# A two-layer transformer kernel: the per-layer embedding product computed in the opening and kept in device memory, and x turned by products with a diagonal

## The reference

```python
cs = silu(c); mod = cs @ w_ada + b_ada              # shift1, scale1, ... of 1024 each
h = rms_norm(x, norm1_g) * (1 + scale1) + shift1     # rms_norm scales a row by 1/sqrt(mean(x*x)+eps)
proj = h @ w_in                                      # first layer: queries, keys, values, gates
...
x = x + mixed @ w_o                                  # second layer, "out2"
h2 = rms_norm(x, norm_mlp)
x = x + square(relu(h2 @ w_up)) @ w_down             # second layer, "mlp"
gate = sigmoid(rms_norm(x, norm_ple) @ w_ple_gate)
x = x + gate * (p_l @ w_ple)                         # p_l: 512 x 256, w_ple: 256 x 1024
```

## Time and profile before

| what | value |
|---|---|
| median of 3 runs | 2037.22 us (2035.78 to 2039.25) |
| the profiled execution | 2035.74 us |
| its span | 2033.9 us |
| PE busy | 1983.1 us, 97% |
| DVE, ACT, POOL busy | 1071.8, 805.8, 95.8 us |
| first of the 40 slices, PE busy | 6 tenths |
| the chain that ended last | PE 88%, DVE 6%, ACT 3%, DMA 1% |
| moved by DMA | 195.65 MB, 291 and 321 GB/s in slices 1 and 2, mean 96 |

### The profile page before, as it was taken

The page is one execution under the profiler, slowest core; times in us unless marked ns, Lnnn a source line. Parts: engine busy times, 40 slices in busy tenths (PEclk is TensorE's granted clock), DMA queues, the critical chain, the costliest instruction groups (busy, mean ns, idle before and its releaser), DMA issues.

```text
span 2033.9 us, 24084 instructions
## 1 busy us (share of the span) xinstructions
PE 1983.1 (97%) x9148; PEld 1599.4 (79%) x9148; DVE 1071.8 (53%) x1669; ACT 805.8 (40%) x1341; POOL 95.8 (5%) x116
## 2 busy tenths in 40 slices
PE   6999999999999999999999999999999999999998
PEld 4778777888888888877777777777778888888887
DVE  6686867456443544556363535666654453443355
ACT  4343556534221343333232323577742432322242
POOL 0140000011000000200000000000000100000010
PEclk9999999999999999999999999999999999999999
DMA  8842222123323332332322221212132233323221
GB/s 291 321 165 84 63 72 74 63 86 86 103 79 101 91 102 78 109 102 64 98 68 91 74 89 55 64 48 61 42 104 93 85 102 104 103 82 103 93 93 63
DMA packets 196487, 195.65 MB, mean 96 GB/s; under 512 B 8192, under 2 KB 170616, under 8 KB 194360
## 3 DMA queue, kind: packets, MB, share of 16 engines
q1 hardware_dynamic: 192928, 174.88, 27.9%
q0 software_dynamic: 3280, 19.67, 2.5%
q10 hardware_dynamic: 200, 0.06, 0.0%
HBM read 192.50 MB, written 2.10 MB: 96 GB/s over the span
## 4 chain that ended last, share of the span: by engine, by line
PE 88%; DVE 6%; ACT 3%; DMA 1%; issue 1%; SPq 0%; DVEq 0%; ACTq 0%
PE bank L735 45%; PE bank L700 4%; PE bank L1224 4%; PE bank L974 4%; PE bank L813 4%; PE bank L799 3%; PE bank L1477 3%; PE bank L1297 3%; PE bank L1029 2%; PE bank L1201 2%; PE bank L958 1%; PE bank L1212 1%; PE bank L924 1%; PE bank L1244 1%; PE bank L1164 1%
## 5 line engine op out<-in xcount | busy, mean ns | idle before, releaser
L1601 ACT ACTIVATE w_hi<-raw 128x2048 fp32r<-128x2048 f32 (+4 forms) x165 | 285.6, 1731 | 435.3 <-PE bank L735 300.6
L2357 DVE TENSOR_TENSOR w_lo<-raw,w_hi 128x2048 fp32r<-128x2048 f32 (+4 forms) x163 | 337.3, 2069 | 162.4 <-ACT w_hi L1601 160.6
L735 PE MATMUL bank<-h_hi,w_hi 128*128 128x512 f32 x864 | 338.5, 392 | 3.4 <-DVE w_lo L2357 3.4
L735 PE MATMUL bank<-h_hi,w_lo 128*128 128x512 f32 x864 | 337.1, 390 | 0.0
L735 PE MATMUL bank<-h_lo,w_hi 128*128 128x512 f32 x864 | 336.8, 390 | 0.0
L735 PEld LDWEIGHTS bank<-h_hi,w_hi 128*128 128x128 f32 x864 | 162.6, 188 | 38.4 <-DVE w_lo L2357 2.7
L735 PEld LDWEIGHTS bank<-h_lo,w_hi 128*128 128x128 f32 x864 | 162.6, 188 | 34.4 <-issue 0.5
L735 PEld LDWEIGHTS bank<-h_hi,w_lo 128*128 128x128 f32 x864 | 162.5, 188 | 34.0
L735 PE MATMUL bank<-u_hi,w_hi 128*128 128x512 f32 x256 | 100.9, 394 | 0.0
L735 PE MATMUL bank<-u_hi,w_lo 128*128 128x512 f32 x256 | 100.4, 392 | 0.0
L735 PE MATMUL bank<-u_lo,w_hi 128*128 128x512 f32 x256 | 99.4, 388 | 0.0
(11 more groups left out here) (543 smaller groups left out, 4092.4 us busy)
## 6 DMA issues: line engine op xcount, KB each, us to landing
raw<-in_w_in SPq DMA_DIRECT2D x49, 1024.0 KB
raw<-in_w_ff SPq DMA_DIRECT2D x44, 512.0 KB
raw<-in_w_up SPq DMA_DIRECT2D x16, 1024.0 KB
raw<-in_w_down SPq DMA_DIRECT2D x16, 1024.0 KB
raw<-in_w_o SPq DMA_DIRECT2D x8, 1024.0 KB
raw<-in_w_br SPq DMA_DIRECT2D x8, 1024.0 KB
raw<-in_w_in SPq DMA_DIRECT2D x13, 512.0 KB
raw<-in_w_ff SPq DMA_DIRECT2D x8, 768.0 KB
```

The lines of the kernel that those rows point to most:

```text
L735: last = nc.tensor.matmul(dst, a, b, start=k == n == 0, stop=k == last_k and n == 2)
L1601: nc.scalar.activation(w_hi[:, slot, 0:width], raw[:, slot, 0:width], ACT.Copy).then_inc(hi_done, 1)
L2357: v.tensor_tensor(w_lo[:, slot, 0:width], raw[:, slot, 0:width], w_hi[:, slot, 0:width].bitcast(F32), ALU.subtract).then_inc(lo_done, 1)
```

## The change

The two units of `ple_in` become units 0 and 1 of the program, ahead of `values`; everything before `mlp` gets numbers higher by two. SP loads p (0.5 MB) and both halves of `w_ple` (1 MB) directly behind c and ahead of x. TensorE transposes p, multiplies the first half (`ple_half(0)`), turns feature tiles 0 to 3 of x, multiplies the second half, and only then does `columns(0)`. ScalarE and VectorE split p and the two units before they turn to x and `w_ada`. Seven of the eight results are copied by ScalarE and one by VectorE; GpSimd stores them to a device memory tensor `ple_kept` in two transfers of 1 MB, and loads all 2 MB back into `aret` when the second layer's `merge2` has ended. p and its parts now lie in unused halves of the ring's slots.

x is no longer scaled before it is turned. ScalarE scales the 128x128 identity by the row factors of each 128 tokens instead, giving four diagonal blocks, and `turn_x` is a float32 product of x with such a block in place of a transpose.

In `mlp` the 48 products, the eight transposes of p and the copies are gone. `norm_sum(2)` stands behind the first unit of the first quarter, the first quarter is unrolled, its second unit is split earlier, and VectorE's eight multiplications of x by `mean2` stand half in the second and half in the third round of the quarter.

```diff
```diff
             def prologue():
-                sp.dma_start(crow[:], A["c"][0, :].rearrange("(r n) -> r n", n=P)).then_inc(sem("c_in"), 16)
+                sp.dma_start(crow, A["c"][0, :].rearrange("(r n) -> r n", n=P)).then_inc(sem("c_in"), 16)
+                sp.dma_start(p_in, A["p_2"][0, 0].rearrange("(t p) n -> p t n", p=P)).then_inc(sem("p_loaded"), 16)
+                w_p = rows(A["w_ple_2"][0])
+                for half in range(2):
+                    load(U0["ple_in"] + half, half, [(slot_view(half, 2, 512), w_p[:, :, 512 * half:512 * half + 512])])
                 sp.dma_start(x_in[:], A["x"][0].rearrange("(t p) n -> p t n", p=P)).then_inc(sem("x_in_done"), 16)
                 for hf in range(2):
                     for k in range(KD):
...
             def ple():
-                pool.wait_ge(mm_done, U0["out2"])
-                nc.gpsimd.dma_start(p_in[:], A["p_2"][0, 0].rearrange("(t p) n -> p t n", p=P)).then_inc(sem("p_in_done"), 16)
+                pool.wait_ge(sem("merged"), 2 * KD)
+                nc.gpsimd.dma_start(aret[:], ple_kept).then_inc(sem("p_in_done"), 16)
+
+            def ple_keep():
+
+                pool.wait_ge(sem("p_copied"), 4)
+                nc.gpsimd.dma_start(ple_kept[:, 0:4, :], xT[:, 4:8, :]).then_inc(sem("ple_saved"), 16)
+                pool.wait_ge(sem("p_copied"), 7)
+                pool.wait_ge(sem("p_made"), 3)
+                nc.gpsimd.dma_start(ple_kept[:, 4:8, :], ple_b[:]).then_inc(sem("ple_saved"), 16)
 
             prologue()
+            ple_keep()
             modulation_loads()
             distances()
```

More of the change, by code:

```diff
@@ L74 @@
 STAGES = [
+    ("ple_in", [1024] * 2),
     ("values", [2048] * 4),
@@ L87 @@
     ("out2", [2048] * 4),
-    ("ple_in", [1024] * 2),
     ("mlp", [2048] * 32),
@@ L200, in two_layers @@
         vrows = sbuf("vrows", [P, P], at=start)
-        crow = sbuf("crow", [KD, P], at=start)
+        crow = xT[0:KD, 0, 0:P]
         lrow = sbuf("lrow", [1, 4 * D_A], at=start)
@@ L204, in two_layers @@
         lsum = sbuf("lsum", [1, 8], at=start)
+        ple_b = sbuf("ple_b", [P, 4, S], at=start)
         start.close()
@@ L297, in two_layers @@
         mla_out.close()
-        p_in = sbuf("p_in", [P, QT, 256])
-        p_hi = sbuf("p_hi", [P, 2, S], F32R)
-        p_lo = sbuf("p_lo", [P, 2, S], F32R)
+        p_in = raw[:, 0, UW // 2:UW].rearrange("p (t n) -> p t n", t=QT)
+        p_hi = w_hi[:, 1, UW // 2:UW].rearrange("p (k n) -> p k n", k=2)
+        p_lo = w_lo[:, 1, UW // 2:UW].rearrange("p (k n) -> p k n", k=2)
+        ple_kept = nc.dram_tensor("ple_kept", (P, KD, S), F32).ap()
+        diag = [att[:, 0:P], att[:, P:2 * P], junk[:, 0, :], junk[:, 1, :]]
         u_hi = sbuf("u_hi", [P, KD, S], F32R)
@@ L530, in mlp @@
                                                  w_down[:, ds(i * KD, KD), 256 * k:256 * k + 256])])
-            def ple_in():
-                w_p = rows(A["w_ple_2"][0])
-                for half in range(2):
-                    load(U0["ple_in"] + half, half, [(slot_view(half, 2, 512), w_p[:, :, 512 * half:512 * half + 512])])
             def ple():
@@ L1638, in mlp_ring @@
                 u0 = U0["mlp"]
-                body(0, u0, lambda u, k: split(u + k))
+                body(0, u0, lambda u, k: None if k == 1 else split(u + k))
                 with act.Fori(1, 3) as i:
@@ L1689, in prologue @@
                 nc.scalar.activation(lsum[0:1, 2:4], lsum[0:1, 0:2], ACT.Exp).then_inc(sem("small_exp"), 1)
-                split(1)
+                split(3)
                 high1(1)
@@ L1720, in values @@
             def values():
-                split(2)
-                split(3)
+                split(4)
+                split(5)
+                act.wait_ge(sem("ple_saved"), 32)
                 for n, dst in enumerate((va, vb)):
@@ L2437, in prologue @@
                     v.reduce_sum(lsum[0:1, n:n + 1], ldot[0:1, n, :], axis=AX).then_inc(sem("dve_small"), 1)
+                dve.wait_ge(mm_done, U0["ple_in"] + 2)
+                v.tensor_copy(ple_b[:, 3, :], bank[3][:]).then_inc(sem("p_made"), 1)
                 make_h1(0)
-                split(0)
+                split(2)
                 chunk(0, 1)
@@ L3258, in mlp @@
             def mlp():
-                u = U0["ple_in"]
-                split(u + 1)
                 low(2, G_MLP, KD - 2, KD)
-                split(u + 2)
+                split(U0["mlp"] + 1)
                 def body(i, u, nxt):
```

33 lines of the change are left out of this document (9 added, 24 removed).

## The result

| | median of | us | span of the profiled execution | profiled execution |
|---|---|---|---|---|
| before | 5 runs | 2037.22 (2033.16 to 2039.25) | 2033.9 | 2035.74 |
| changed | 5 runs | 2024.99 (2024.37 to 2026.99) | 2025.2 | 2026.99 |

The two profiled executions lie 8.75 us apart.

The account below looks back on a forecast made before the run. TensorE, busy 97% of the span, was taken as the bound. Removing 11.9 us at the end and losing 6.1 in the opening gave -5.8, so 2029.9 from the profile or 2031.4 from the median; forecast 2030.6 us, range 2027 to 2036.

Parts of the forecast that it names:

- The end: Between out2 and mlp: 48 products (10.99 us) and eight transposes (0.87) leave the chain, 11.86 us, with no new wait.
- rival D: At the start of mlp: an unseen wait costs 3 us of the gain, 2033.6; chance 0.10.
- the cover that I gave them: At the start of mlp: VectorE's and ScalarE's steps finish in time, with 4 us of slack.
- The opening's TensorE: Opening: TensorE's added products and turning set the pace, so values starts at 34.9 instead of 27.64, 7.3 us later.
- +6.1 forecast: Opening's net loss: 7.3 later, less 2.2 for warm values, plus 1.0 for turning tiles 6 and 7.
- Rival B: Opening: bound by transfers, first half at full clock, loss only 2.9 us, 2027.4; chance 0.08.
- C's slow clock: Opening: TensorE stays at 1.2 GHz throughout, values 19.8 us late, +8.9 in all, 2045; chance 0.10.
- the writes and the transfers: Opening: the two 1 MB writes could hold back w_ada by between 0 and 2.2 us; taken as 0.
- the -5.8 of the sum: Whole kernel: -11.9 at the end and +6.1 in the opening give -5.8 us.
- buys nothing: Opening clock: by the rows transposes counted as well, so replacing them with products leaves the clock's fall its chance.
- charged the diagonal with 1.0 us: Turning tiles 6 and 7: eight blocks by products instead of transposes, 8 x (0.23 - 0.11) = 1.0 us slower.
- Rival A: Opening: the clock falls ahead of values or the writes hold back w_ada, costing 2.2 us, 2032.8; chance 0.22.

Follow-up runs that it names:

- experiments 3 and 4: Kernel before and changed kernel, each with GpSimd's fifth w_ada load held until the index unit's weights landed: 2031.57 us (ratio 0.9975) and 2024.81 us (0.9941).
- experiment 8: Changed kernel plus 16 identity products in TensorE's early idle time and GpSimd's fifth w_ada load held until the index unit's weights landed: 2025.01 us, ratio 0.9945.
- the third profiles of both: Repeat profiles with no edit: kernel before 2039.51 us, changed kernel 2025.15 us.
- experiment 2: Kernel before with only x turned by float32 products with diagonal blocks instead of transposes: 2037.25 us, ratio 1.0006.
- the load is spaced: Changed kernel with x scaled whole and transposed, and GpSimd's fifth w_ada load held until the index unit's weights landed: 2026.88 us, ratio 0.9961.
- the second profile of before: Repeat profile of the kernel before with no edit: 2034.60 us.

## Why the prediction was wrong

**The end: right.** -11.86 was forecast. Before, the 48 products began at 1613.51. In the changed kernel the first sum of norm_sum begins at 1626.66 behind a unit of mlp (48 x 0.229 = 11.0 us), so mlp began at 1615.7: 2.2 us later, which is the +2.6 in front less 0.87 for the transposes of p, plus 0.5 lost somewhere between queries and out2 that I did not trace. 2.2 - 10.99 = -8.8, the difference of the whole: nothing is lost behind. No wait stands at mlp: rival D is out. VectorE's and ScalarE's steps had the cover that I gave them.

**The opening's TensorE: right, step by step.** First product 13.24 (13.3), first half 7.88 us (7.7, with the low clock at its start), turning 3.57 (3.7), second half 5.49 (5.5), columns from 30.02 (30.2) to 31.9 (32.1), values at 34.67 (34.9), the first sixteen of them 3.90 us instead of 5.87, and the turning of tile 6 between them 0.89 instead of 0.44. +6.1 forecast, +5.96 measured. Here the transfers were later than I had them (x_in took 11.9 us and ScalarE waited 1.33 for it), but not by enough to be in front of TensorE: VectorE's sums ended at 28.1 us, 1.9 before TensorE asked. Rival B needed it the other way round, and C's slow clock ended at 17.65 us.

**The step that failed** is that of the writes and the transfers: "I take 0, since the chain behind 27.64 is PE's and not a transfer's". The chain of before did run over a transfer, "61.47 16.80 DMA raw<-in_w_in", with a wait of 2.3 us and 1.9 us of low clock behind it. I read the chain's first 200 us for the opening and its end for mlp, wrote "from there PE carries the chain", and took the stretch between to move as a block. It didn't: TensorE came to the index unit 6.8 us later (87.12 against 82.59 less 2.3; 6.0 from the opening, 0.9 from low clock at 59 to 65 us), while the load's weights came only 3.5 us later (81.78 against 78.29), and 2.3 of wait and 1.9 of low clock disappeared. The load was issued 6.0 us later as well (67.50 instead of 61.47), but it took 14.3 us instead of 16.8. Had it taken 16.8 again, 1.5 us of the wait would have stayed. In the three profiles of the changed kernel it took 13.6 to 14.3 us, in the three of before 15.5 to 18.3; GpSimd's next loads are issued 1.5 us behind it in both, and why it was shorter stays open. Removing the wait in both kernels (experiments 3 and 4) brings the distance to -6.8, near the -5.8 of the sum. In that pair of profiles columns(1) begins 4.5 us later (53.02 and 57.53) and not 6.1, and the rest is 11.2 shorter.

The rest of the miss in the medians is of another kind. They lie 12.2 us apart, the profiled executions 8.75: before's is 1.5 under its median, and that of the changed kernel is the slowest of its five, 2.0 above its median, with 1.6 lost in the second layer (experiment 8). Besides, before has an opening that varies: columns at either clock (1.96 or 3.59 us), values from 27.64 to 29.89, and a wait at the index unit of 1.0 to 3.1 us, behind which the 48 products took 0.3 to 3.1 us more than 10.88. I took the sum from the profile with the earliest values, where the change has most to lose. In the third profiles of both, columns(1) begins at 53.64 and 57.57, 3.9 us later and not 6.0, and the index unit's 48 products end at 100.82 and 97.67, 3.2 us sooner: that pair lies 14.4 us apart in the end.

**The clock.** I said that by the rows the replacement of transposes buys nothing, and charged the diagonal with 1.0 us. By itself in before the time doesn't change (experiment 2). In the changed kernel it is worth 10.4 us (2035.40 against 2024.99), of which 8.5 go when the load is spaced (2026.88) and some 2 stay (2026.88 against 2024.81, intervals overlapping). Two things lie in it. ScalarE's 4.27 us become 1.3 us on the path to TensorE; and the first sixteen products of values take 3.8 to 3.9 us in all seven profiles in which x is turned by products, but 5.5 to 6.2 in six of the seven with transposes (in the seventh the clock had fallen earlier, at 23 us, and was back). That is some 2 us for the 0.9 that the products cost in tiles 6 and 7, so "buys nothing" was wrong.

The Trainium skill (TensorE: Matmul & The Clock Gate, Part 4: PE-mode transpose) says that transposes don't bring the clock up, and by it a low clock in values is less likely with products. These counts are on its side. It doesn't hold strictly: of the five profiles with the opening of before, columns ran at the full clock, 1.96 us, in two, behind nothing but transposes. And products don't keep a fall away: in experiment 2 the clock fell at columns behind them as well.

Rival A stayed out: the clock at 32 to 34 us was 1.00, and the writes delayed nothing that TensorE asked for by then.

## What to carry to other kernels

When a change delays an engine, go down the chain to the next row that belongs to another engine or a transfer: the wait that stands there, with the low clock behind it, can shrink or go, and is a term of the sum. Ask whether that transfer is issued later by as much, as it was here, and how much its duration varies between profiles: here by more than the wait. An engine's single wait on a load that shares the queues with bulk loads of another engine is worth a try at once: one wait on GpSimd gave 4.2 us here. And look at more than one profile of the kernel before when its runs spread over 6 us: the profile from which I summed was its most favourable opening.

## What was unexpected in the hardware

- A 1 MB load took 13.6 to 19.0 us from issue to landing in the ten profiles in which it ran beside 1 MB loads of GpSimd, and 8.5 and 8.1 us in before and in the changed kernel once these were held. In before its weights were there 6.4 us earlier (71.89 against 78.29), though it was issued 1.9 us later. Beside them it varies between executions of one kernel: 15.5, 16.8 and 18.3 us in before. By the two queues' rows above, GpSimd's loads moved in packets of 7.3 KB on average and SP's in packets of 0.5 KB.
- A wait of 2.3 to 4.0 us on TensorE at full load was followed by the low clock: the 48 products behind it took 12.80 us after 2.3, 13.99 after 3.1, 13.77 after 3.6 and 13.53 after 4.0, against 10.88 with none. After 0.3, 0.9 and 1.0 us they took 11.17 or 11.18, and the granted clock stayed at 1.00.
- The granted clock of the windows does not tell of every slow stretch. In the changed kernel the windows show 1.00 from 12 to 56 us, while the first products stand 0.43 us apart. In the second profile of before they show 1.00 from 20 to 34 us too, where columns took 3.59. Timeline of TensorE in the changed kernel:

```profile
17.22 0.63 PE L710 MATMUL bank<-w_hi 128*128 128x512 f32 x1
17.65 0.48 PE L710 MATMUL bank<-w_lo,w_hi 128*128 128x512 f32 x1
17.96 0.40 PE L710 MATMUL bank<-w_hi,w_lo 128*128 128x512 f32 x1
18.20 0.40 PE L710 MATMUL bank<-w_hi 128*128 128x512 f32 x1
```

  The distances between starts, 0.43 and then 0.24 us, are the two levels, 1.2 and 2.4 GHz; the change came 4.4 us behind the first product.
- The clock also falls some 1.5 ms into a busy program, after a gap of 2.3 us between norms and products, in 6 of 14 profiles, and twelve products behind it take 4.34 us instead of 2.77. The gap is as long in the profiles without the fall.
